# Two-block fp32 forward pass: attention sources normed beside the preceding projections, and the state-space mixer's sines and coefficients made beside the MLP and the input projection

## The chip, the cores and the metric

One core of a Trainium2 chip runs one program. The metric is the device time of one execution in microseconds, the median of several runs. The core has TensorE (PE; PEld are its weight loads), VectorE (DVE), ScalarE (ACT), GpSimd (POOL) and SyncE (SP), each with its own instruction stream; they meet through semaphores. 16 DMA engines move data between HBM and the on-chip memory SBUF. Matmul results land in PSUM.

## The reference, cut to what matters

Two blocks over 256 tokens of width 2048. The first is a mixer of long convolutions and a state-space scan with a squared-ReLU MLP (2048 to 8192 to 2048). The second, where the change lies:

```python
hn = rms_norm(h, norm_mix_g)
proj = hn @ w_in                                  # 2048 -> 3 x 1024: conv_a, conv_gate, ssm_u
yc = conformer_conv_group(conv_a, conv_gate, ...) # GLU, causal depthwise conv of 31 taps, norm, silu
ys = s5_group(ssm_u, lam_re, lam_im, log_dt, b, c, d, glu_w)
#   dt = exp(log_dt); lam_bar = exp(lam * dt); b_bar = ((lam_bar - 1) / lam) * b
#   states: scan of  s[t] = lam_bar * s[t-1] + b_bar u[t];  y = Re(c s) + d u;  gelu, gate
h = h + concat(rms_norm(yc), rms_norm(ys)) @ w_out
hn, mem_n = rms_norm(h, norm_mem_g), rms_norm(mem, mem_norm_g)
h = h + mem_cross_attention(hn, mem_n, w_q, w_kv, w_o)
h = h + peer(rms_norm(h, norm_ffn_g), ...)        # 16384 experts, top 16 of 8 heads
```

## The kernel before, in words

Activations lie feature-major: 16 tiles (KD) of 128 features by 256 tokens (T). A matmul keeps fp32 accuracy by splitting weights and activations into a rounded part and a rest (hi, lo).

`linear_stage` (line 603) is the dense stage. Per output tile there are 16 weight blocks of 128x128 in 4 quarters (a quarter is 128x512). SP streams 512 KB pairs of quarters into a ring of 4. ScalarE rounds a quarter into one of 4 slots (`make_hi`, L195) once TensorE has used the slot (`multiplied`); VectorE subtracts for the rest (`make_lo`, L202); TensorE multiplies (L793). So TensorE has at most four quarters, one tile, ahead. `split_and_take` sets the order on ScalarE and on VectorE: for tile n, first the four quarters of tile n + 1, then `take` of tile n, then the quarters of tile n + 2. In `take`, ScalarE copies half of the sum out of PSUM (L707), VectorE adds the other (L763) and runs `finish`: in the MLP's first layer a squared ReLU and its split (L1493 to L1495), after output projections x += and the sum of squares (L2202, L248, L249). Stages are separate blocks, with all engines meeting between them. A layer with `source` has its activations split first (L699, L751), one with `norm` also scaled (L726, L733), ahead of the first matmuls.

A `Beside` object is side work. Its hooks are called at fixed points: `tensor`, `scalar` and `after_tile` after each tile, `after_split(q)` after each `make_lo`, `last_vector` after the last tile, `issue` on GpSimd's queue. A layer with such an object is written out instead of looped. `split_and_take` counts quarters as `i * per + g`, with i the round of the layer and g from 4; each layer of a stage has a `split_and_take` of its own.

The second block in order: `in2` (8 + 8 + 8 tiles, the middle ones with a Sigmoid on ScalarE), `s5_setup_stage` (line 1507: exponentials, sines and some forty VectorE steps for the scan's coefficients b, c, r and turn), `local_mixers_stage` (line 1597), `glu`, group norm, `mix2_out`, `mem_q`, `mem_k`, values, attention, `mem_out`, experts. `mem_q` also loads mem and lets GpSimd sum its squares (`sum_tiles`, L595, L598) for `mem_k`'s norm.

In `local_mixers_stage`, for each of 8 tiles f: ScalarE makes phases (L1632, L1634), later their Sine (L1656), and 31 diagonal matrices of the convolution's taps (L1643); VectorE brings phases to one turn (L1719, L1720), rotates the inputs (L1737 to L1741), scans (L1748), rotates back with cosines (L1755), GpSimd with sines (L1622); TensorE makes inputs (L1673), outputs (L1687) and the 31 taps (L1698), in the order taps 0 to 11, inputs(f + 1), outputs(f - 1), taps 12 to 30.

Of the kernel before, what the change touches and what calls it, by code (L numbers as in the profile page):

```python
# [62 lines left out]
TWO_PI = 6.283185  # L63

# [60 lines left out]
class Core:  # L125


    def __init__(self, nc, ctx, dram):
# [8 lines left out]
        self.small = self.sb("small", [P, 4])  # L137
        self.mod = self.sb("mod", [P, 6 * KD, 2])
# [8 lines left out]
        self.moved, self.summed, self.shaped = (self.sem(f"tile_{n}") for n in ("moved", "summed", "shaped"))  # L147
        self.source_rounded, self.source_split = self.sem("source_rounded"), self.sem("source_split")
# [292 lines left out]

class ModulationBeside(Beside):
# [160 lines left out]
def linear_stage(core, name, layers, next_w, loads=(), begin_next=True, squares_of=None, beside=None):  # L603
# [21 lines left out]
    with ExitStack() as own:  # L625
# [42 lines left out]
        @block.gpsimd  # L668
        def _(pool):
            if beside is not None:  # L670
                beside.issue(pool)
            if squares_of is not None:
                pool.wait_ge(loaded, 16 * len(loads))
                sum_tiles(core, pool, loads[0][0], *squares_of)

# [268 lines left out]
def sine_steps(core, dve, x, k, bound_done):  # L944

    magic = 12582912.0
    c1, c2 = 6.28125, 2 * math.pi - 6.28125
    step = lambda ins: core.dve.step(dve, ins)
    step(dve.tensor_scalar(k, x, 1 / (2 * math.pi), magic, ALU.mult, ALU.add))
    step(dve.tensor_scalar(k, k, -magic, None, ALU.add))  # L950
    step(dve.scalar_tensor_tensor(x, k, -c1, x, ALU.mult, ALU.add))
    step(dve.scalar_tensor_tensor(x, k, -c2, x, ALU.mult, ALU.add))
    dve.tensor_scalar(x, x, 3.1415925, -3.1415925, ALU.min, ALU.max).then_inc(bound_done, 1)

# [7 lines left out]
def filter_stage(core, dft, filters):  # L962
# [6 lines left out]
    with ExitStack() as own:  # L969
# [10 lines left out]
        with nc.Block() as block:  # L980
# [61 lines left out]
            def _(dve):  # L1042
                step = lambda ins: core.dve.step(dve, ins)
                for n, bias in enumerate((b1, b2)):
# [4 lines left out]
                    sine_steps(core, dve, x, k, s["bounded"])  # L1049
# [372 lines left out]
def first_block(core):  # L1422
# [62 lines left out]
    with nc.sbuf_tensor("mlp_parts", [P, KD, 2, T], F32R) as parts:  # L1485
# [4 lines left out]
        with nc.sbuf_tensor("hidden", [P, MLP_TILES, 2, T], F32R) as hidden:  # L1490
            def squared_relu(dve, n, slots):
# [8 lines left out]
                    for c in range(chunks)]  # L1500
            linear_stage(core, "mlp", [Layer("w_mlp1", MLP_TILES, [parts], finish=squared_relu, steps=2), *down],
                         ("w_in_2", 0))
# [4 lines left out]
def s5_setup_stage(core, s5):  # L1507

    nc, dram = core.nc, core.dram
    s = {n: core.sem(f"s5_{n}") for n in ("loaded", "c_loaded", "cleared", "dt", "rate", "exp", "bounded", "sine")}
    W = HT * 64
    with ExitStack() as own:
        sb = lambda name, shape: own.enter_context(nc.sbuf_tensor(f"s5_{name}", shape, F32))
        rep = sb("rep", [P, 5, W])
        dt, e, trig, k = sb("dt", [P, W]), sb("e", [P, W]), sb("trig", [P, 2, W]), sb("k", [P, 2, W])
        kr, ki, t1, t2, inv = (sb(n, [P, W]) for n in ("kr", "ki", "t1", "t2", "inv"))
        sdt = sb("sdt", [P, PAIRS])
        sk = sb("sk", [P, PAIRS])  # L1520
        with nc.Block() as block:
            @block.sync
            def _(sp):
                sp.dma_start(rep[:], dram["s5_rep"]).then_inc(s["loaded"], 16)
                sp.wait_ge(s["cleared"], 1)

                for g in range(2):
                    for part in range(2):
                        sp.dma_start(s5.c[g * 64:(g + 1) * 64, part, :, g * 16:(g + 1) * 16],
                                     dram["s5_c"][part, g * 64:(g + 1) * 64]).then_inc(s["c_loaded"], 16)  # L1530

            @block.scalar
            def _(act):
                act.activation(sdt[:], core.prm["log_dt"], ACT.Exp).then_inc(s["dt"], 1)
                act.wait_ge(s["loaded"], 16)
                act.activation(dt[:], rep[:, 2, :], ACT.Exp).then_inc(s["dt"], 1)
                act.wait_ge(s["rate"], 1)
                act.activation(s5.r[:], s5.r[:], ACT.Exp)
                act.wait_ge(s["rate"], 2)
                act.activation(e[:], e[:], ACT.Exp).then_inc(s["exp"], 1)  # L1540
                act.wait_ge(s["bounded"], 1)
                act.activation(trig[:], trig[:], ACT.Sin).then_inc(s["sine"], 1)

            @block.vector
            def _(dve):
                step = lambda ins: core.dve.step(dve, ins)
                mul = lambda out, a, b: step(dve.tensor_tensor(out, a, b, ALU.mult))
                dve.memset(s5.c[:], 0.0).then_inc(s["cleared"], 1)
                dve.wait_ge(s["dt"], 1)
                dve.tensor_tensor(s5.r[:], core.prm["lam_re"], sdt[:], ALU.mult).then_inc(s["rate"], 1)  # L1550
                mul(s5.turn[:], core.prm["lam_im"], sdt[:])

                step(dve.tensor_scalar(s5.turn[:], s5.turn[:], 1 / (2 * math.pi), None, ALU.mult))
                step(dve.tensor_scalar(sk[:], s5.turn[:], MAGIC, None, ALU.add))
                step(dve.tensor_scalar(sk[:], sk[:], -MAGIC, None, ALU.add))
                step(dve.tensor_tensor(s5.turn[:], s5.turn[:], sk[:], ALU.subtract))
                dve.wait_ge(s["dt"], 2)
# [39 lines left out]
def local_mixers_stage(core, s5, proj, conv):  # L1597
# [8 lines left out]
    with ExitStack() as own:  # L1606
# [8 lines left out]
        with nc.Block() as block:  # L1615
# [9 lines left out]
            def _(act):  # L1625
# [28 lines left out]
                for f in range(HT):  # L1654
# [6 lines left out]
                    if f + 1 < HT:  # L1661
                        make_diag(f + 1)
# [788 lines left out]
```

## Time and profile before

| what | us |
|---|---|
| median of 3 runs (range) | 4411.7 (4409.6 to 4418.7) |
| profiled execution, whole | 4409.9 |
| its span | 4408.1 |
| MLP, first layer (64 tiles) | 357.8 |
| in2, first to last matmul (24 tiles) | 136.5 |
| from there to the mixers' first matmul | 35.9 |
| local mixers | 179.2 |
| mix2_out, first to last matmul (16 tiles) | 90.9 |
| mem_q, from mix2_out's last matmul to its own | 119.6 |
| mem_k, the same | 101.4 |

The table's stages are windows of one profiled execution. A row of a timeline gives start, duration, engine, line, operation, output and inputs; equal neighbours are merged (x8). "[0.75 <-PE ps L793]" is idle time before it and what ended it; PEq is a start of a stage. A group's busy time is not its cost: an engine that is not the limit of its stage may idle freely.

### The profile page before, as it was taken

The numbers are of one execution on the slowest core, as the hardware profiler recorded it, in microseconds if no ns is written. First come the engines' busy times: TensorE is split into PE (matmuls) and PEld (weight loads), VectorE is DVE, ScalarE is ACT, GpSimd is POOL, SyncE is SP. The second block draws the span as 40 slices with busy tenths as digits, with TensorE's granted clock in tenths as the row PEclk, the third lists the DMA queues.
The fourth block names the chain that finished last, engine by engine and source line by source line (L and its number), as shares of the span: only waits on it lengthen the run. The fifth ranks groups of instructions, "written<-read, shape, count | busy, mean of one in ns | idle before, by whom it ended". The sixth has DMA issues, their size and how long they took to land. (4 is left out here: it accounts for less than half of the span.)

```text
span 4408.1 us, 67179 instructions
## 1 busy us (share of the span) xinstructions
PE 3929.2 (89%) x21628; PEld 3230.7 (73%) x21628; DVE 2812.7 (64%) x5152; ACT 2086.3 (47%) x3815; POOL 172.7 (4%) x192
## 2 busy tenths in 40 slices
PE   6799968668999999858788999998889999999998
PEld 0466744557888888747577778877678888888887
DVE  0653445677777667669676556688776666666667
ACT  0442320234555555548544434444765555555554
POOL 3011100000000000002101000000000000000000
PEclk9899979888999999979898999899999999999999
DMA  9686710025666666430154545465246666666665
GB/s 335 233 302 242 263 60 0 1 91 149 190 190 187 189 190 186 140 106 1 39 180 144 167 138 154 152 188 180 77 137 205 205 204 187 189 187 189 189 188 161
DMA packets 203369, 717.71 MB, mean 163 GB/s; under 512 B 30263, under 2 KB 30296, under 8 KB 202456
## 3 DMA queue, kind: packets, MB, share of 16 engines
q1 hardware_dynamic: 181240, 633.41, 46.1%
q0 software_dynamic: 21984, 82.41, 5.2%
q8 instruction: 85, 1.39, 0.1%
q14 instruction: 60, 0.49, 0.0%
HBM read 707.35 MB, written 8.39 MB: 162 GB/s over the span
## 5 line engine op out<-in xcount | busy, mean ns | idle before, releaser
L202 DVE TENSOR_TENSOR weights_lo<-ring,weights_hi 128x512 fp32r<-128x512 f32 x2240 | 1522.6, 690 | 1025.3 <-ACT weights_hi L195 1011.3
L195 ACT ACTIVATE weights_hi<-ring 128x512 fp32r<-128x512 f32 x2240 | 1401.3, 631 | 1405.2 <-PE ps L793 1340.6
L793 PE MATMUL ps<-expert_parts,weights_hi 128*128 128x512 f32 x4224 | 1465.6, 394 | 34.5 <-DVE weights_lo L202 27.0
L793 PE MATMUL ps<-expert_parts,weights_lo 128*128 128x256 f32 x4224 | 1140.8, 280 | 0.0
L793 PEld LDWEIGHTS ps<-expert_parts,weights_hi 128*128 128x128 f32 x4224 | 780.1, 188 | 205.6 <-issue 36.5
L793 PEld LDWEIGHTS ps<-expert_parts,weights_lo 128*128 128x128 f32 x4224 | 796.6, 189 | 20.4
L793 PE MATMUL ps<-mlp_parts,weights_hi 128*128 128x512 f32 x1024 | 353.6, 394 | 16.0 <-PEq L552 16.0
L793 PE MATMUL ps<-hidden,weights_hi 128*128 128x512 f32 x1024 | 351.2, 392 | 0.0
L793 PE MATMUL ps<-att_parts,weights_hi 128*128 128x512 f32 x768 | 271.0, 400 | 29.6 <-DVE att_parts L751 28.1
L793 PE MATMUL ps<-h_parts,weights_hi 128*128 128x512 f32 x704 | 268.9, 409 | 10.0 <-DVE weights_lo L202 10.0
L793 PE MATMUL ps<-mlp_parts,weights_lo 128*128 128x256 f32 x1024 | 276.9, 281 | 0.0
L793 PE MATMUL ps<-hidden,weights_lo 128*128 128x256 f32 x1024 | 275.9, 280 | 0.0
L793 PEld LDWEIGHTS ps<-mlp_parts,weights_hi 128*128 128x128 f32 x1024 | 188.8, 189 | 54.7 <-issue 16.7
L793 PEld LDWEIGHTS ps<-hidden,weights_hi 128*128 128x128 f32 x1024 | 187.7, 188 | 37.6
L793 PE MATMUL ps<-att_parts,weights_lo 128*128 128x256 f32 x768 | 209.9, 283 | 0.0
L793 PEld LDWEIGHTS ps<-mlp_parts,weights_lo 128*128 128x128 f32 x1024 | 193.5, 189 | 5.4
L372 PE MATMUL ps<-ada_ring,silu_c 128*32 128x512 f32 x768 | 150.6, 628 | 51.5 <-DMA ada_ring<-in_w_ada 51.1
L793 PEld LDWEIGHTS ps<-hidden,weights_lo 128*128 128x128 f32 x1024 | 192.3, 188 | 5.4
L793 PE MATMUL ps<-h_parts,weights_lo 128*128 128x256 f32 x704 | 194.5, 285 | 0.0
L793 PEld LDWEIGHTS ps<-h_parts,weights_hi 128*128 128x128 f32 x704 | 134.9, 192 | 74.6 <-issue 45.0
L793 PEld LDWEIGHTS ps<-att_parts,weights_hi 128*128 128x128 f32 x768 | 144.0, 192 | 61.2 <-issue 32.3
L793 PEld LDWEIGHTS ps<-att_parts,weights_lo 128*128 128x128 f32 x768 | 147.6, 192 | 4.0
(440 smaller groups left out, 4859.0 us busy)
## 6 DMA issues: line engine op xcount, KB each, us to landing
ring<-in_w_mlp SPq DMA_DIRECT2D x256, 512.0 KB, 3.6
ring<-in_w_u SPq DMA_DIRECT2D x256, 512.0 KB, 4.2
ring<-in_w_v_tab SPq DMA_DIRECT2D x256, 512.0 KB, 3.7
ada_ring<-in_w_ada POOLq DMA_DIRECT2D x124, 512.0 KB, 6.3
ring<-in_w_mix SPq DMA_DIRECT2D x88, 512.0 KB, 5.4
ada_ring<-in_w_ada SPq DMA_DIRECT2D x68, 512.0 KB, 5.3
ring<-in_w_out SPq DMA_DIRECT2D x64, 512.0 KB, 3.7
ring<-in_w_in SPq DMA_DIRECT2D x48, 512.0 KB, 3.7
```

The costliest lines, as they stand in the source:

```text
L195: act.activation(core.hi[:, g % SLOTS], core.ring[:, slot, at:at + QUARTER], ACT.Copy).then_inc(core.rounded, 1)
L202: dve.tensor_tensor(core.lo[:, g % SLOTS], core.ring[:, slot, at:at + QUARTER], core.hi[:, g % SLOTS].bitcast(F32), ALU.subtract).then_inc ...
L372: mm = pe.matmul(self.core.ps[32 * j:32 * j + 32, self.bank(part), :], self.cond[:, k, :], self.ring[:, slot, (j % 2) * BANK:(j % 2 + 1) * ...
L793: mm = pe.matmul(out, part[:, g % SLOTS, k, :], moving, start=at == 0 and part is core.hi, stop=last and part is core.hi)
```

## The change

- `TurnsBeside` makes the mixers' sines beside the MLP's first layer (64 tiles): on even turns ScalarE makes the phases of one of 32 pairs, on odd turns VectorE rounds and subtracts and ScalarE takes the Sine; GpSimd's queue stores them to HBM, and the mixers' SP queue loads them per f.
- `MixerSetup` replaces `s5_setup_stage` and runs beside `in2`. GpSimd issues its loads (c in 16 parts) and clears c. `vector_first` and `vector_second` are generators spread over quarters by `after_split`.
- In the mixers VectorE makes the 31 diagonals of f = 0, ScalarE the rest; phases and Sine are gone from the stage.
- `NormBeside` makes a normed and split source beside another stage: that of mem (load, GpSimd squares, norm) beside `mix2_out` from tile 5, that of x beside `mem_k`. `mem_k` now runs ahead of `mem_q`, and neither has a source to make. Attention's scratch moves into an unused buffer.

```diff
+class NormBeside(Beside):
+    def tensor(self, pe, t):
+        if t == self.at:
+            if self.squared is not None:
+                pe.wait_ge(self.squared, 1)
+            pe.matmul(self.core.ps[:, self.BANK, 0:T], self.core.ones[:], self.squares, start=True,
+                      stop=True).then_inc(self.done["summed"], 1)
+    def scalar(self, act, turns):
+        t = turns[0] - self.at
...
+        if 2 <= t < 2 + KD // 2:
+            two = slice(2 * (t - 2), 2 * (t - 2) + 2)
+            act.wait_ge(self.done["scaled"], self.pairs + t - 1)
+            act.activation(self.parts[:, two, 0, :], self.scaled[:, two, :], ACT.Copy).then_inc(self.done["rounded"], 1)
+    def after_tile(self, dve, n):
+        t = n - self.at
...
+        if 1 <= t < 1 + KD // 2:
+            for k in (2 * (t - 1), 2 * (t - 1) + 1):
+                ins = dve.scalar_tensor_tensor(self.scaled[:, k, :], self.src[:, k, :], self.gain[:, k:k + 1], self.std,
+                                               ALU.mult, ALU.mult)
+            ins.then_inc(self.done["scaled"], 1)
+        if 3 <= t < 3 + KD // 2:
+            two = slice(2 * (t - 3), 2 * (t - 3) + 2)
+            dve.wait_ge(self.done["rounded"], self.pairs + t - 2)
+            dve.tensor_tensor(self.parts[:, two, 1, :], self.scaled[:, two, :], self.parts[:, two, 0, :].bitcast(F32),
+                              ALU.subtract)
...
+class TurnsBeside(Beside):
+    def issue(self, pool):
+        for u in range(PAIRS):
+            pool.wait_ge(self.done["trig"], u + 1)
+            pool.dma_start(self.saved[u // 4, :, u % 4], self.trig[:, u % 2]).then_inc(self.kept[u % 2], 16)
...
+    def scalar(self, act, turns):
+        n, small = turns[0], self.core.small
+        u = n // 2
+        if n % 2 == 0 and 0 <= u < PAIRS:
+            if u == 0:
+                act.wait_ge(self.done["rate"], 1)
+            if u >= 2:
+                act.wait_ge(self.kept[u % 2], 16 * (u // 2))
...
+        if n % 2 == 1 and 0 <= u < PAIRS:
+            act.wait_ge(self.done["phase"], u + 1)
+            act.activation(self.trig[:, u % 2], self.trig[:, u % 2], ACT.Sin, scale=TWO_PI).then_inc(self.done["trig"], 1)
+    def make_phase(self, dve, u):
...
+        dve.tensor_scalar(first, phases[:, 0], MAGIC, -MAGIC, ALU.add, ALU.add)
+        dve.tensor_scalar(second, phases[:, 1], MAGIC, -MAGIC, ALU.add, ALU.add).then_inc(done["step"], 1)
+        dve.wait_ge(done["step"], u + 5)
+        dve.tensor_tensor(phases[:, 0], phases[:, 0], first, ALU.subtract)
+        dve.tensor_tensor(phases[:, 1], phases[:, 1], second, ALU.subtract).then_inc(done["phase"], 1)
...
+class MixerSetup(Beside):
+    PART_A, PART_B = (2 * SLOTS, 10 * SLOTS), (12 * SLOTS, 22 * SLOTS)
+    COLUMNS_A, COLUMNS_B = 8400, 26000
...
+    def scalar(self, act, turns):
+        s = self.done
+        if 1 in turns:
+            act.wait_ge(s["loaded"], 16)
+            act.activation(self.dt[:], self.rep[:, 2, :], ACT.Exp).then_inc(s["dt"], 1)
+        if 10 in turns:
+            act.wait_ge(s["rate"], 2)
+            act.activation(self.s5.r[:], self.s5.r[:], ACT.Exp)
+            act.activation(self.e[:], self.e[:], ACT.Exp).then_inc(s["exp"], 1)
+            act.wait_ge(s["bounded"], 1)
+            act.activation(self.trig[:], self.trig[:], ACT.Sin).then_inc(s["sine"], 1)
+    def after_split(self, dve, q):
...
+        (a, b), (c, d) = self.PART_A, self.PART_B
+        if a <= q < b:
+            while self.spent * (b - a) < (q + 1 - a) * self.COLUMNS_A:
+                self.spent += next(self.first, self.COLUMNS_A)
...
+        if c <= q < d:
+            while self.spent * (d - c) < (q + 1 - c) * self.COLUMNS_B:
+                self.spent += next(self.second, self.COLUMNS_B)
+    def last_vector(self, dve):
+        for _ in self.second:
+            pass
...
@@ local_mixers_stage
-                make_turns(0)
-                make_diag(0)
+                make_diag(1)
...
+                for k in range(CONV31):
+                    dve.tensor_scalar(diag[:, 0, k, :], core.cst["ident"], core.prm["conv_w"][:, k:k + 1], None,
+                                      ALU.mult).then_inc(s["first_diag"], 1)
...
@@ second_block
-            ], ("w_glu", 0))
+            ], ("w_glu", 0), beside=MixerSetup(core, s5, sb3))
...
+            linear_stage(core, "mix2_out", [Layer("w_out_2", KD, [parts], finish=onto_stream(core), source=h, squares=True, steps=3)],
+                         ("w_k", 0), loads=[(mem[:], "mem")], squares_of=(mem_squares[:], mem_sum[:]),
+                         beside=NormBeside(core, mem, mem_sum[:, 0, :], core.prm["mem_norm"], mem_std[:], mem,
+                                           mem_parts, at=5, squared=core.loaded_squared))
...
+        linear_stage(core, "mem_k", [Layer("w_k", KD, [mem_parts], into=lambda n: k[:, n, :])], ("w_q", 0),
+                     beside=NormBeside(core, core.x, core.squares, core.prm["norm_mem"], std[:], h, parts))
+        linear_stage(core, "mem_q", [Layer("w_q", KD, [parts], into=lambda n: q[:, n, :])], ("w_v", 0))
```

## Rows read from the trace of the kernel before

**Rows 1.** the page, engines: busy us, share, instructions.

```profile
PE 3929.2 (89%) x21628; PEld 3230.7 (73%) x21628; DVE 2812.7 (64%) x5152; ACT 2086.3 (47%) x3815; POOL 172.7 (4%) x192
```

**Rows 2.** windows: length, busy by engine, clock, DMA share, GB/s.

```profile
1048.90:1406.70 357.80, 357.80 (x2048) 314.41 (x2049) 259.59 (x507) 178.70 (x318) 0.00 (x0) 0.99 0.61 188
1788.90:1925.40 136.50, 136.19 (x768) 119.07 (x768) 81.46 (x138) 77.91 (x135) 0.00 (x0) 0.98 0.58 177
1925.40:1961.30 35.90, 0.00 (x0) 0.02 (x1) 31.01 (x45) 6.14 (x10) 0.00 (x0) 0.53 0.30 51
1961.30:2140.50 179.20, 144.57 (x880) 113.29 (x880) 143.65 (x130) 144.71 (x328) 36.20 (x8) 0.89 0.00 1
2210.80:2301.70 90.90, 90.82 (x512) 79.54 (x512) 69.19 (x126) 45.29 (x81) 0.00 (x0) 0.98 0.60 182
2301.70:2421.30 119.60, 94.94 (x514) 81.93 (x514) 78.08 (x105) 49.32 (x85) 17.08 (x5) 0.87 0.48 158
2421.30:2522.70 101.40, 92.35 (x515) 80.27 (x514) 62.21 (x102) 49.35 (x85) 0.00 (x0) 0.95 0.52 166
2840.00:3123.00 283.00, 259.28 (x1440) 219.23 (x1438) 225.90 (x612) 127.94 (x270) 5.92 (x11) 1.00 0.60 188
```

**Rows 3.** timeline, one MLP tile: start, us, engine, line, op.

```profile
1201.49 0.63 ACT L195 ACTIVATE weights_hi<-ring 128x512 fp32r<-128x512 f32 x1 [0.75 <-PE ps L793]
...
1204.23 0.42 DVE L1495 TENSOR_TENSOR hidden<-mlp_sums,hidden 128x256 f32 x1
...
1204.57 1.29 DVE L202 TENSOR_TENSOR weights_lo<-ring,weights_hi 128x512 fp32r<-128x512 f32 x2
...
1207.05 0.63 ACT L195 ACTIVATE weights_hi<-ring 128x512 fp32r<-128x512 f32 x1 [0.76 <-PE ps L793]
```

**Rows 4.** timeline, start of the values stage.

```profile
2525.09 0.79 PE L1870 MATMUL ps<-weights_hi,att_parts 128*128 128x512 f32 x1 [2.38 <-PEq L625]
```

**Rows 5.** timeline, start of mem_q.

```profile
2308.28 3.26 DVE L733 SCALAR_TENSOR_TENSOR h_att<-x,params,mem_q_rstd 128x256 f32<-128x256 f32 x8
...
2312.59 12.66 DVE L733 SCALAR_TENSOR_TENSOR h_att<-x,params,mem_q_rstd 128x256 f32<-128x256 f32 x4
...
2313.14 7.20 POOL L595 TENSOR_TENSOR mem_squares<-mem 128x4096 f32<-128x4096 f32 x1 [176.54 <-DMA mem<-in_mem]
...
2325.17 3.36 DVE L751 TENSOR_TENSOR att_parts<-h_att,att_parts 128x1024 fp32r<-128x1024 f32 x1
```

**Rows 6.** timeline, gates, VectorE.

```profile
3132.86 1.11 DVE L2195 TENSOR_SCALAR gates_right<-consts,turned 128x128 f32<-128x128 f32 x4
```

**Rows 7.** waits of TensorE, experts_first: total, times, longest.

```profile
PE ps L793 <- DVE weights_lo L202: 23.6, 36, 1.3
```

**Rows 8.** timeline, ScalarE, a table load.

```profile
2826.03 1.28 ACT L2257 ACT_TABLE_LOAD   x1
```

**Rows 9.** timeline, end of in2 and the s5 setup, VectorE.

```profile
1926.70 0.41 DVE L763 TENSOR_TENSOR proj<-proj,ps 128x256 f32<-128x256 f32 x1
...
1939.86 1.41 DVE L1547 TENSOR_TENSOR s_t<-s_rep 128x512 f32<-128x512 f32 x2
...
1960.32 0.69 DVE L1591 TENSOR_SCALAR s_cc<-s_cc 128x1024 f32<-128x1024 f32 x1
```

**Rows 10.** timeline, local mixers.

```profile
1977.31 7.92 PE L1698 MATMUL ps<-mix_c,mix_diag 128*128 128x256 f32 x24 [13.90 <-ACT mix_diag L1643]
...
2023.51 12.02 ACT L1643 ACTIVATE mix_diag<-consts,small,params 128x128 f32<-128x128 f32 x31
...
2042.29 1.15 PE L1673 MATMUL ps<-proj,s_b 32*128 32x256 f32 x16
...
2045.23 8.47 PE L1698 MATMUL ps<-mix_c,mix_diag 128*128 128x256 f32 x38
...
2049.04 1.20 DVE L1719 TENSOR_SCALAR mix_p<-mix_trig 128x2048 f32<-128x2048 f32 x1
...
2050.27 2.29 DVE L1720 TENSOR_TENSOR mix_trig<-mix_trig,mix_p 128x2048 f32<-128x2048 f32 x1
```

More of the change, by code:

```diff
@@ L1500, in first_block @@
                     for c in range(chunks)]
-            linear_stage(core, "mlp", [Layer("w_mlp1", MLP_TILES, [parts], finish=squared_relu, steps=2), *down],
-                         ("w_in_2", 0))
+            with ExitStack() as beside:
+                turns = TurnsBeside(core, lambda name, shape: beside.enter_context(nc.sbuf_tensor(name, shape, F32)),
+                                    core.trig_saved)
+                linear_stage(core, "mlp", [Layer("w_mlp1", MLP_TILES, [parts], finish=squared_relu, steps=2), *down],
+                             ("w_in_2", 0), beside=turns)
@@ L1615, in local_mixers_stage, with _ @@
         with nc.Block() as block:
+            @block.sync
+            def _(sp):
+                for f in range(HT):
+                    if f >= 2:
+                        sp.wait_ge(s["out_c"], f - 1)
+                        sp.wait_ge(s["out_s"], f - 1)
+                    sp.dma_start(trig[:, f % 2], core.trig_saved[f]).then_inc(trig_landed[f % 2], 16)
             @block.gpsimd
@@ L1875, in values_stage, with attention_stage @@
     core.begun = True
[L1878 removed]
+def attention_stage(core, q, k, v, out, space):
     nc, ps = core.nc, core.ps
@@ L2238, in second_block @@
             glu_stage(core, y, parts, ("w_out_2", 0))
-        with nc.sbuf_tensor("out2_parts", [P, KD, 2, T], F32R) as parts, nc.sbuf_tensor("h_out2", [P, KD, T], F32) as h:
-            group_norm_stage(core, conv[:], y, h)
-            linear_stage(core, "mix2_out", [Layer("w_out_2", KD, [parts], finish=onto_stream(core), source=h, squares=True, steps=3)], ("w_q", 0))
-    with ExitStack() as attention:
-        sb = lambda name, shape, dt=F32: attention.enter_context(nc.sbuf_tensor(name, shape, dt))
-        q, k, v = sb("q", [P, KD, T]), sb("k", [P, KD, T]), sb("v", [P, TT, 4, BANK])
-        parts, h, mem = sb("att_parts", [P, KD, 2, T], F32R), sb("h_att", [P, KD, T]), sb("mem", [P, KD, T])
-        mem_squares, mem_sum = sb("mem_squares", [P, KD, T]), sb("mem_sum", [P, 1, T])
-        linear_stage(core, "mem_q", [Layer("w_q", KD, [parts], into=lambda n: q[:, n, :], source=h,
-                                         norm=Norm(core.x, core.prm["norm_mem"], squares=core.squares))], ("w_k", 0),
-                     loads=[(mem[:], "mem")], squares_of=(mem_squares[:], mem_sum[:]))
-        linear_stage(core, "mem_k", [Layer("w_k", KD, [parts], into=lambda n: k[:, n, :], source=mem,
-                                         norm=Norm(mem, core.prm["mem_norm"], squares=mem_sum[:, 0, :]))], ("w_v", 0))
-        values_stage(core, parts, v, ("w_o", 0))
-        attention_stage(core, q, k, v, parts)
```

308 lines of the change are left out of this document (191 added, 117 removed).

## The prediction

> **What bounds the kernel now.** I read the page's engine totals first, then busy time in windows whose edges are TensorE's first and last matmuls of a stage, then the order of instructions inside them. The total names the engine: TensorE is busy 89% of the span [rows 1]. The windows say where it is not the limit [rows 2]. In the MLP it is busy without a break, one tile of 16 weight blocks per 5.56 us (from one last rounding of a tile to the next, 1201.49 to 1207.05 [rows 3]); there, work on VectorE or ScalarE costs nothing until it makes the weight halves late. Four stretches are not of that kind: the s5 setup (1925.4 to 1961.3, TensorE at 0), the local mixers (179.2 us, 144.6 busy), and the starts of mem_q and mem_k (119.6 and 101.4 us for 16 tiles that take 16 x 5.56 = 89.0). Each part of the change shortens one of these and loads a dense stage instead, so I cost both sides. The profiled execution took 4409.9 us (span 4408.1), the median of the three runs 4411.7: I sum on the first and carry the difference over.
>
> **1. Attention sources (mem_q and mem_k).** Removed: the norm and split ahead of both stages. Their excess over 89.0 us is 30.6 + 12.4 = 43.0 us [rows 2]. Left is a plain hand-over: TensorE stood 2.4 us before the values stage, which has no source to make [rows 4], and a little longer, say 3.6, after a stage with x += and squares. A stage that starts after such a pause is 1.8 us (mix2_out, 90.9 - 89.0) to 3.1 us (in2, 136.5 - 24 x 5.56) over its steady pace; 2.6 each. So 3.6 + 2.4 + 5.2 = 11.2 remain, and 31.8 us go.
> Added in mix2_out, first the sum of squares of mem on GpSimd. It now runs beside VectorE's weight splits. In mem_q it held VectorE up: four scalings take 12.66 us while GpSimd's square and its first addition run, against 3.26 for the eight before, and a split of 1024 columns takes 3.36 against twice 0.69 for two of 512 (my reading: one VectorE instruction gets through per GpSimd instruction) [rows 5]. GpSimd is busy 17.1 us in five instructions [rows 2]. The load of mem leads the stage's queue as before, so the square starts as late as there, 7.8 us after a hand-over (2313.14 [rows 5] against 2301.7 + 3.6), in TensorE's first or second tile. VectorE gets some five instructions in 17 us and needs seven such ones per tile; TensorE has four weight quarters (5.56 us) ahead. Followed through: the third quarter of tile 1 is 3 us late, the fourth 3 more, the first of tile 2 4 to 5 more, which makes 11 us, and one restart at half clock, 2.6: 13.5 us (8 to 17; if these splits were not held, 0). Whether a split of 512 columns is held like the rows' forms, no row shows.
> The Trainium skill, page "SBUF — State Buffer", section "Who interferes with whom", says that a VectorE instruction with two SBUF inputs is shut out for the whole of a GpSimd instruction that reads SBUF. The two held forms agree with it; by it the splits, x += and the squares are held too, and the sum of a PSUM tile is not, which is how I took it.
> Second, NormBeside's VectorE work: per tile 2 scalings (0.41 each, 3.26 / 8) and one 512-column subtraction (0.69), 1.6 us onto 69.2 / 16 = 4.3, so 5.9 to 6.1 against 5.56 for the six tiles that hold both: 3 us (0 to 6). In mem_k, without x += and squares, the same load is under the pace: 0. Part 1: -31.8 + 13.5 + 3 = -15 us (-24 to -8).
>
> **2. Sines beside the first MLP layer (TurnsBeside).** Per pair of tiles: on an even turn ScalarE makes two phases; on the odd turn VectorE rounds and subtracts them after its own finish, and ScalarE waits for that ("phase"), then does a Sine of 128x512. Queued behind this wait on ScalarE is the rounding of the first weight quarter of the tile after next; behind that, VectorE's split and TensorE. In [rows 3] TensorE ends a tile at 1201.4, VectorE's finish at 1204.65, the split of the quarter in question at 1205.2, and TensorE needs it at 1207.0: 1.8 us spare. Now, after 1204.65: two adds of 128x256 (at least 0.26, which a 128x128 form takes in a row [rows 6], at most 0.42, as the subtraction; I take 0.3), two subtractions (0.36 to 0.42), and 0.05 for each hand-over: 1.35, to 1206.0; Sine 0.63 (ScalarE's time for 512 columns, L195 [rows 3]) to 1206.6; rounding 0.63; split 0.69: 1207.95. Late by 0.95 us, 32 times: 30 us, and 2.6 once for the rate chain in tile 0 and the first Sine's table load: 33 us (0.65 to 1.25 each: 23 to 43). The next tile has no such wait and does not win it back, since TensorE has no faster pace. That this coupling exists is seen in experts_first, where ScalarE's Gelu waits for VectorE in the same way: TensorE waits for weight halves 36 times, 23.6 us, longest 1.3 [rows 7], at a granted clock of 1.00 [rows 2]. The 32 saves on GpSimd's queue (256 KB each) hold no one: a slot is wanted again three tiles, 16.7 us, later.
>
> **3. Input projection (MixerSetup).** The first generator (6.5 us of VectorE over tiles 2 to 7, beside 3.2 per tile) fits. But its first step waits for ScalarE's exponential, which stands behind ScalarE's take of tile 1; queued behind VectorE's wait is the split of quarter 9: 1.7 us once. On turn 10 ScalarE does three activations (32, 512 and 1024 columns, 1.9 us by the 0.63 of 512) and two table loads of 1.28 [rows 8] between the sigmoid and the next rounding: 4.4 us against some 2.1 of cover, 2.3 us. Sum +4 (2 to 8).
> The table load's row is 1.28 us with no idle time before it [rows 8]. The Trainium skill, "ScalarE: Activation LUTs", section "What ACT_TABLE_LOAD costs", adds a drain of about 1.38 us to each switch; by it this part would be some 3 us more. The row shows no drain; I keep the row.
> The second generator is the surprise of the diff. It is meant for quarters 48 to 88, but the number that after_split gets is `i * per + g`, which starts again in each layer: with 8 tiles of 4 quarters it never passes 31. So part B is never met, and last_vector runs the whole second generator after the last tile, with nothing beside it. In the setup these steps stand from 1939.86 to 1961.01 [rows 9]: 21.15 us, which stay on the path. What goes is the stage change, the clearing, the load and the first half: 35.9 us from TensorE's last matmul to its next become 1.7 (to 1927.1, the end of the last take [rows 9]) + 21.15 + 0.3: -12.7 us (-14 to -10).
>
> **4. Local mixers.** Removed from ScalarE: 8 phases and one Sine per f; what is left is 12.0 of diagonals and 0.5 [rows 10]. VectorE loses 1.20 + 2.29 [rows 10] of 143.7 / 8 = 18.0 [rows 2] and keeps 14.5. TensorE's own cycle is 31 taps at 8.47 / 19 = 0.446, 13.8, and 2.94 for inputs and outputs (2042.29 to 2045.23): 16.8, now the longest. Start: the first diagonals move to VectorE, 31 after the 2.5 us product. At 0.26 each [rows 6] the first eight are there at 4.6 us, all at 10.5. Taps begin at 4.7 instead of 16.0 (1977.31 [rows 10]), and 12 of them take 7.9 at half clock, to 12.6; inputs(1) wait for VectorE's two products of 2.29, to 15.0; with inputs and 19 taps f = 0 ends at 24.7; seven more of 16.8 make 142.3; last outputs and skip 3.7: 146 against 179.2: -33 us (-37 to -25). The stored sines come by the SP queue, 1 MB per f, issued 10 us and more before they are wanted.
>
> **Sum.** -15 + 33 + 4 - 12.7 - 33 = -23.7: 4386.2 for the profiled execution, 4388.0 as a median.
>
> **Rivals.** (a) The Sine costs nothing: if VectorE's additions end 1 us sooner than I put together, part 2 is 3 and the time 4358. For: 1.8 us spare; against: a chain of four operations that adds up to 2.75. (b) Slower: the recurring pauses in the MLP drop TensorE's clock. Deciding point: a pause over 1.3 us, which left the clock at 1.00 in experts_first, up to the 2.4 after which the first matmul took 0.79 instead of 0.39 [rows 4]. If each of the 32 did, 2.6 us more each: +83, 4471. Against: my pause is 0.95. (c) GpSimd's squares do not hold the 512-column splits: 13.5 less, 4374.5. (d) The change does what it says and the coefficients lie inside the loops: -21.15, but ScalarE-bound sigmoid tiles with a VectorE step per quarter give back some 7.5: 4374.
>
> **How the numbers follow.** Forecast as summed, 0.72; (a) 0.10; (b) 0.06; (c) 0.08; (d) 0.04. A measurement of this kernel can tell 0.2% (8.8 us) from no change: the forecast case's own ends (the five ranges seldom all on one side) are 4370 to 4408, and 0.09 of it lies within 8.8 us of no change. Faster by over 0.2%: 0.84, within: 0.09, slower: 0.07. The range takes in (a), (c), (d) and a dearer part 2 and leaves (b) out: 4358 to 4412.
>
> **What would show it.** MLP up: TensorE's window 385 to 395 us instead of 357.8, its waits named on weights_lo, about 1 us, 32 times, ScalarE idle before Sine for VectorE. Before the mixers: about 23 us without a matmul, VectorE busy on s_t, s_kr, s_ki. Mixers about 146 us, no wait for mix_diag after f = 0. mix2_out about 105 us with a VectorE instruction of some 7 us; mem_k and mem_q some 95 each. It is wrong if the MLP window is under 370 or over 400, if coefficient steps stand among the splits of the input projection, or if mix2_out stays at 91.

## The result, and the profile after

The changed kernel takes 4372.1 us (median of four, 4369.1 to 4375.7) against 4411.1 for the kernel before: a ratio of 0.9908, with a 95% interval of 0.9895 to 0.9921. The forecast was 4388.0, in a range of 4358 to 4412. The profiled execution took 4375.7 us, span 4373.9, so the profiles differ by 34.2 us where the medians differ by 39.

Windows of the changed kernel (length, then busy time of TensorE, its weight loads, VectorE, ScalarE and GpSimd, then granted clock, DMA share, GB/s). In order: first MLP layer, input projection, the pause before the mixers, mixers up to the first matmul of the gated linear unit, mix2_out.

```profile
1047.00:1434.80 387.80, 366.02 (x2049) 314.50 (x2050) 292.39 (x637) 214.36 (x416) 16.85 (x31) 0.99 0.61 195
...
1818.20:1960.60 142.40, 138.34 (x768) 120.68 (x768) 87.21 (x146) 77.86 (x136) 9.54 (x15) 0.97 0.58 176
1960.60:1984.00 23.40, 0.31 (x5) 0.29 (x8) 21.49 (x32) 1.19 (x3) 0.00 (x0) 0.56 0.00 0
1984.00:2131.30 147.30, 136.40 (x881) 108.86 (x880) 123.61 (x147) 92.29 (x229) 36.33 (x8) 0.95 0.17 60
...
2195.40:2299.80 104.40, 95.72 (x514) 82.23 (x514) 94.07 (x150) 49.88 (x89) 16.98 (x5) 0.93 0.54 177
```

The mixers' window ends at another edge than that of [rows 2]. With the same edge the kernel before has:

```profile
1961.30:2146.80 185.50, 144.57 (x880) 113.29 (x881) 145.12 (x132) 149.91 (x332) 36.20 (x8) 0.89 0.01 3
```

Stretch by stretch:

| stretch | before | after | difference | forecast |
|---|---|---|---|---|
| first MLP layer | 357.8 | 387.8 | +30.0 | +33 |
| input projection | 136.5 | 142.4 | +5.9 | +4 |
| last matmul before the mixers to their first | 35.9 | 23.1 | -12.8 | -12.7 |
| mixers, to the gated linear unit | 185.5 | 147.6 | -37.9 | -33 |
| mix2_out | 90.9 | 104.4 | +13.5 | +16.5 |
| end of mix2_out to the first matmul of values | 223.4 | 189.6 | -33.8 | -31.8 |
| sum | | | -35.1 | -24.0 |

(The prediction rounds part 1 up to -15 and so sums to -23.7.) All the rest of the span differs by 0.9. What was given is seen in three places of the trace. First the MLP: a timeline of ScalarE, VectorE and TensorE over one odd tile (start, us, engine, line; in brackets the idle time before and what ended it).

```profile
1208.83 0.42 DVE L1554 TENSOR_TENSOR hidden<-mlp_sums,hidden 128x256 fp32r<-128x256 f32 x1
1209.17 0.29 DVE L1634 TENSOR_SCALAR params<-turn_trig 128x256 f32<-128x256 f32 x1
1209.37 0.28 DVE L1635 TENSOR_SCALAR turn_whole<-turn_trig 128x256 f32<-128x256 f32 x1
1209.69 0.43 DVE L1637 TENSOR_TENSOR turn_trig<-turn_trig,params 128x256 f32<-128x256 f32 x1
1210.04 0.42 DVE L1638 TENSOR_TENSOR turn_trig<-turn_trig,turn_whole 128x256 f32<-128x256 f32 x1
1210.49 0.63 ACT L1607 ACTIVATE turn_trig<-turn_trig 128x512 f32<-128x512 f32 x1 [3.27 <-DVE turn_trig L1638]
1211.03 2.18 ACT L200 ACTIVATE weights_hi<-ring 128x512 fp32r<-128x512 f32 x4
...
1211.44 0.40 PE L846 MATMUL ps<-mlp_parts,weights_hi 128*128 128x512 f32 x1
...
1211.67 2.50 DVE L207 TENSOR_TENSOR weights_lo<-ring,weights_hi 128x512 fp32r<-128x512 f32 x4 [1.22 <-ACT weights_hi L200]
1212.51 0.48 PE L846 MATMUL ps<-mlp_parts,weights_hi 128*128 128x512 f32 x1 [0.67 <-DVE weights_lo L207]
...
1212.83 0.28 PE L846 MATMUL ps<-mlp_parts,weights_lo 128*128 128x256 f32 x1
```

ScalarE stands idle for 3.27 us with four weight quarters to round, VectorE then for 1.22 with four to split, TensorE for 0.67. The waits over the whole layer (total, times, longest), TensorE's and ScalarE's, say that this is the rule:

```profile
PE ps L846 <- DVE weights_lo L207: 21.8, 32, 0.9
...
ACT turn_trig L1607 <- DVE turn_trig L1638: 100.3, 31, 3.3
```

Second, mix2_out, timeline of VectorE and GpSimd: three splits of 512 columns, of which two take 1.29 us in [rows 3], take 15.02 us while GpSimd makes its square and first additions.

```profile
2200.56 7.02 POOL L647 TENSOR_TENSOR mem_squares<-mem 128x4096 f32<-128x4096 f32 x1 [79.40 <-DMA mem<-in_mem]
2200.81 15.02 DVE L207 TENSOR_TENSOR weights_lo<-ring,weights_hi 128x512 fp32r<-128x512 f32 x3 [1.08 <-ACT weights_hi L200]
2207.65 9.33 POOL L650 TENSOR_TENSOR mem_squares<-mem_squares 128x2048 f32<-128x2048 f32 x3
2208.18 0.50 PE L846 MATMUL ps<-out_parts,weights_hi 128*128 128x512 f32 x1 [3.90 <-DVE weights_lo L207]
...
2209.32 0.61 PE L846 MATMUL ps<-out_parts,weights_hi 128*128 128x512 f32 x1
...
2213.12 0.80 PE L846 MATMUL ps<-out_parts,weights_hi 128*128 128x512 f32 x1 [2.98 <-DVE weights_lo L207]
...
2215.76 0.41 DVE L816 TENSOR_TENSOR mix_out_sums<-mix_out_sums,ps 128x256 f32<-128x256 f32 x1
```

Third, the pause before the mixers and their start, timeline of VectorE and TensorE. L1723 is the second generator's first step:

```profile
1962.29 1.41 DVE L1723 TENSOR_TENSOR s_t<-s_rep 128x512 f32<-128x512 f32 x2
...
1983.74 2.09 PE L1844 MATMUL ps<-proj,s_b 32*128 32x256 f32 x16 [23.09 <-PEq L677]
...
1986.14 6.15 DVE L1898 TENSOR_SCALAR mix_diag<-consts,params 128x128 f32<-128x128 f32 x31
...
1996.74 1.20 PE L1844 MATMUL ps<-proj,s_b 32*128 32x256 f32 x16 [1.94 <-DVE mix_p L1905]
1997.87 15.24 PE L1872 MATMUL ps<-mix_c,mix_diag 128*128 128x256 f32 x62
...
2015.98 13.66 PE L1872 MATMUL ps<-mix_c,mix_diag 128*128 128x256 f32 x62
2029.57 1.15 PE L1844 MATMUL ps<-proj,s_b 32*128 32x256 f32 x16
...
2046.09 1.15 PE L1844 MATMUL ps<-proj,s_b 32*128 32x256 f32 x16
```

### The profile page after: what moved, and what is told of

Same layout as the page of the kernel before. It is cut to its first block and busy times, and to the rows that moved or that the text cites. A ratio compares the mean times of both kernels' runs of the same rounds, so it can differ in the third digit from the quotient of the medians.

```text
span 4373.9 us, 65273 instructions
## 1 busy us (share of the span) xinstructions
PE 3928.3 (90%) x21628; PEld 3227.4 (74%) x21628; DVE 2817.6 (64%) x5302; ACT 2062.4 (47%) x3817; POOL 203.9 (5%) x242
## 5 line engine op out<-in xcount | busy, mean ns | idle before, releaser
L846 PE MATMUL ps<-mlp_parts,weights_hi 128*128 128x512 f32 x1024 | 361.5, 397 | 37.6 <-DVE weights_lo L207 21.8
L846 PE MATMUL ps<-att_parts,weights_hi 128*128 128x512 f32 x512 | 176.1, 392 | 4.0 <-PEq L677 2.5
L846 PE MATMUL ps<-in_parts,weights_hi 128*128 128x512 f32 x384 | 136.4, 401 | 11.1 <-DVE in_parts L804 7.1
L846 PEld LDWEIGHTS ps<-h_parts,weights_lo 128*128 128x128 f32 x704 | 135.4, 192 | 8.8
L846 PE MATMUL ps<-att_parts,weights_lo 128*128 128x256 f32 x512 | 138.0, 280 | 0.0
```

Of the source, the lines that this page charges most:

```text
L846: mm = pe.matmul(out, part[:, g % SLOTS, k, :], moving, start=at == 0 and part is core.hi, stop=last and part is core.hi)
```

## The experiments

Each edits the changed kernel and is measured against the kernel before. Three rounds or more give an interval; a kernel with one run is read by its windows.

| kernel | median us | ratio (95%) |
|---|---|---|
| sine_next_turn | 4344.5 | 0.9855 (0.9838 to 0.9871) |
| coefs_in_loops | 4352.9 | 0.9869 (0.9853 to 0.9886) |
| small_mem_sum | 4360.6 | 0.9890 (0.9873 to 0.9906) |
| no_mem_sum | 4359.9 | one run |
| phases_longer | 4427.5 | one run |
| first_taps | 4373.5 | one run |
| coefs_spread | 4345.4 | one run |
| combined_more | 4314.1 | 0.9786 (0.9769 to 0.9802) |
| combined_less | 4307.3 | 0.9767 (0.9753 to 0.9780) |
| combined_moved | 4302.8 | 0.9760 (0.9746 to 0.9773) |

### sine_next_turn: the Sine off the tile that makes its phases

```diff
+        if n % 2 == 0 and u > 0:
+            self.sine(act, u - 1)
         if n % 2 == 0 and 0 <= u < PAIRS:
...
-        if n % 2 == 1 and 0 <= u < PAIRS:
+        if n == 2 * PAIRS - 1:
+            self.sine(act, u)
```

> Each pair's Sine is issued on ScalarE one turn later (turn 2u+2 instead of 2u+1, ahead of that turn's two phases); every instruction of the sines is still there, on the same engines, and the saves too. Theory (the Sine's place: ScalarE waits for VectorE's subtraction inside the same tile, and the rounding of the next weight quarter is queued behind that): the 32 waits of ScalarE for the phase go to nothing but the last, TensorE's waits for weights_lo in the first MLP layer (21.8 us, 32 times) go to under 3 us, its window falls from 387.8 to 358 to 361, and the time from 4372.1 to about 4344. Rival 1 (the added work itself is what the MLP cannot hide, VectorE's 1.2 us and ScalarE's 1.2 us per pair): the window stays at 380 or more. Rival 2 (the 8 MB of saves on GpSimd's queue delay the weight loads): the same, 385 or more, with TensorE's waits led back to DMA.

Measured: TensorE's waits in the layer fell from 21.8 us in 32 to 1.5 in 2, the window to 359.5, the time to 4344.5. Window of the layer:

```profile
1043.00:1402.50 359.50, 358.50 (x2049) 314.89 (x2050) 295.15 (x637) 221.67 (x416) 17.22 (x31) 0.99 0.66 210
```

TensorE's waits in it:

```profile
PE ps L846 <- DVE weights_lo L207: 1.5, 2, 0.9
```

VectorE and ScalarE are as busy as before (295 and 222 us against 292 and 214), and GpSimd's queue stores as much. So the added work and the saves together cost at most 1.7 us (359.5 against 357.8 before): 28 of the 30 us were the place of one wait. Both rivals fall, and rival (a) of the prediction, by which the Sine costs nothing where it stands.

### phases_longer: the same chain made longer

```diff
+        for r in range(5):
+            dve.tensor_scalar(first, phases[:, 0], MAGIC, -MAGIC, ALU.add, ALU.add).then_inc(done["step"], 1)
+            dve.wait_ge(done["step"], 6 * u + r + 5)
         dve.tensor_scalar(first, phases[:, 0], MAGIC, -MAGIC, ALU.add, ALU.add)
...
```

> Ahead of each pair's phases VectorE makes five more rounding steps of 128x256, each waited for by the next (0.29 us and a hand-over of some 0.05 each): the chain from VectorE's finish to ScalarE's Sine grows by 1.5 to 1.7 us, 32 times. Theory (TensorE is late by the chain less a cover that is fixed): its pause of 0.68 us becomes 2.2 to 2.4 us, and the first MLP layer's window 387.8 + 32 x 1.6 = 439 with a clock that stays at 0.99. Rival (b) of the prediction (a pause of more than 1.3 us drops the clock): each restart costs some 2.6 us more, the window passes 500 and the granted clock of the stretch falls under 0.9. If the pauses came from anything else than this chain, the window stays under 400.

Measured, the layer's window:

```profile
1047.30:1490.40 443.10, 370.49 (x2049) 318.32 (x2050) 338.39 (x792) 214.43 (x416) 16.78 (x31) 0.98 0.53 171
```

TensorE's waits in it:

```profile
PE ps L846 <- DVE weights_lo L207: 72.6, 32, 2.3
```

Two restarts in the timeline:

```profile
1208.28 0.47 PE L846 MATMUL ps<-mlp_parts,weights_hi 128*128 128x512 f32 x1 [2.31 <-DVE weights_lo L207]
...
1237.19 0.77 PE L846 MATMUL ps<-mlp_parts,weights_hi 128*128 128x512 f32 x1 [2.32 <-DVE weights_lo L207]
```

A pause grew from 0.68 us (21.8 / 32) to 2.27 (72.6 / 32), by 1.59. The chain from VectorE's finish to its last subtraction took 2.84 us (1203.39 to 1206.23) instead of 1.21, 1.63 more: the cover is fixed and every further us is paid. The window is 443.1 and not the 439 expected, and TensorE is busy 4.5 us longer than in the changed kernel. Some of that is the clock: 31 of the pauses last 2.31 to 2.35 us. After 28 of them the first matmul takes 0.47 us, where steady ones take 0.39, and full clock lasts; two restart at half clock (one at 1237.19, with 0.77 us), and once the clock falls to half 2 us after the restart. Over the layer it is 0.98. Rival (b), by which each such restart costs 2.6 us, is refuted; that such a pause can cost the clock is not.

### small_mem_sum and no_mem_sum: GpSimd's sum of squares in mix2_out

```diff
-    step(pool.tensor_tensor(scratch, src, src, ALU.mult))
+    for k in range(KD):
+        step(pool.tensor_tensor(scratch[:, k, :], src[:, k, :], src[:, k, :], ALU.mult))
...
+    for k in range(2, KD):
+        step(pool.tensor_tensor(out[:, 0, :], out[:, 0, :], scratch[:, k, :], ALU.add))
```

> The sum of squares of mem on GpSimd is made in 31 instructions of 256 columns instead of five of up to 4096 (the same additions but for their order). Theory (while a GpSimd instruction runs, VectorE's split of 512 columns is held until it ends, so one VectorE instruction passes per GpSimd instruction, however long): with 0.5 to 0.7 us per GpSimd instruction a split waits for at most that, VectorE loses some 0.3 to 0.5 us on each of about 20 instructions and not 15 us on three; the window of mix2_out falls from 104.4 to 93 to 97, and the time by 7 to 11 us, to 4361 to 4365. Rival (what counts is GpSimd's busy time, 17 us and now more, in which VectorE runs slower in proportion): the window stays at 102 or more.

```diff
-                sum_tiles(core, pool, loads[0][0], *squares_of)
+                core.pool.step(pool, pool.memset(squares_of[1], 1.0))
```

> The sum of squares of mem is left out: GpSimd fills its result with ones by one small memset, so the attention's keys and values are normed by a constant; the load of mem, NormBeside's own work and all else stay. The window of mix2_out then shows NormBeside's work alone: 91 to 95 us by the theory (the hold costs the rest of the +13.5: I put 13.5 to the hold and 3 to NormBeside), against 100 or more if VectorE's added scalings and subtractions are what costs.

Window of mix2_out in small_mem_sum:

```profile
2189.50:2284.60 95.10, 92.23 (x514) 79.74 (x514) 89.50 (x150) 49.83 (x89) 27.36 (x31) 0.98 0.58 194
```

and in no_mem_sum:

```profile
2196.90:2288.30 91.40, 91.40 (x514) 79.73 (x514) 79.98 (x150) 49.82 (x89) 0.31 (x1) 0.98 0.60 202
```

Without the sum the stage takes 91.4 us: the hold costs 104.4 - 91.4 = 13.0, and NormBeside's own work 0.5 over the 90.9 of [rows 2]. That work leaves VectorE no idle time in the later tiles. From one sum of a tile to that of the fifth tile after it, in no_mem_sum:

```profile
2256.14 0.41 DVE L816 TENSOR_TENSOR mix_out_sums<-mix_out_sums,ps 128x256 f32<-128x256 f32 x1
...
2284.32 0.41 DVE L816 TENSOR_TENSOR mix_out_sums<-mix_out_sums,ps 128x256 f32<-128x256 f32 x1
```

That is 28.18 / 5 = 5.64 us per tile against TensorE's 5.56, and TensorE does not wait.

In small pieces the sum costs 3.7, with the window in the 93 to 97 expected. GpSimd is then busy for 27.4 us instead of 17.0 and VectorE loses less, so it is not GpSimd's busy time that counts but the length of one instruction. Timeline of small_mem_sum beside the pieces:

```profile
2194.36 14.12 POOL L648 TENSOR_TENSOR mem_squares<-mem 128x256 f32<-128x256 f32 x16 [79.16 <-DMA mem<-in_mem]
...
2200.65 4.05 DVE L207 TENSOR_TENSOR weights_lo<-ring,weights_hi 128x512 fp32r<-128x512 f32 x4
2204.62 0.41 DVE L815 TENSOR_TENSOR mix_out_sums<-mix_out_sums,ps 128x256 f32<-128x256 f32 x1
...
2205.53 0.72 DVE L253 TENSOR_TENSOR mix_out_sums<-x 128x256 f32<-128x256 f32 x1
```

Four splits take 4.05 us where they took 2.50 in the MLP; a square of 128x256 with both inputs in SBUF takes 0.72 instead of the 0.43 it takes where no GpSimd instruction runs; the sum whose second input is in PSUM keeps its 0.41. The Trainium skill, "SBUF — State Buffer", section "Who interferes with whom", says that a VectorE instruction with two SBUF inputs contends with a GpSimd instruction that reads SBUF, and one with at most one does not. These rows agree. The x += between them, which has two SBUF inputs as well, took 0.42 to 0.53 in the four tiles: hardly held, and why is open.

### coefs_in_loops, coefs_spread: the second generator into the loops

```diff
     def after_split(self, dve, q):
+        if q < self.passed:
+            self.base += 4 * HT
+        self.passed = q
+        q += self.base
```

> The quarter's number that the setup steps go by is counted on over the three layers of the input projection instead of starting again in each; so the second generator runs on VectorE between the splits of tiles 12 to 21 and not after the last tile. Theory (rival (d) of the prediction): the 23.1 us between the last matmul of the projection and the first of the mixers become 2 to 3, and the projection's window grows from 142.4 to some 150, because a sigmoid tile leaves VectorE little room and a reciprocal of 512 columns (3.3 us) goes between two splits: net -13 us, about 4358. Rival 1 (VectorE's slack of some 2.3 us per tile takes all 21 us over ten tiles): the window stays under 145 and the net is -19 or more, 4352. Rival 2 (stalls that drop TensorE's clock): the window passes 160 and less than 5 us are left of the gain.

coefs_spread adds to that:

```diff
-    PART_A, PART_B = (2 * SLOTS, 10 * SLOTS), (12 * SLOTS, 22 * SLOTS)
+    PART_A, PART_B = (2 * SLOTS, 6 * SLOTS), (12 * SLOTS, 22 * SLOTS)
...
-        if 10 in turns:
+        if 7 in turns:
...
-        step(dve.reciprocal(inv[:], inv[:]))
+        for c in range(4):
+            part = slice(c * W // 4, (c + 1) * W // 4)
+            step(dve.reciprocal(inv[:, part], inv[:, part]))
```

> On top of coefs_in_loops: ScalarE's two exponentials and its Sine come on turn 7, the last tile before the sigmoid layer, instead of turn 10, with the first generator squeezed into tiles 2 to 5, and the reciprocal of 512 columns is made in four instructions of 128 between other splits. coefs_in_loops showed two waits of TensorE that these two should explain: 2.44 us at 1889.94 (turn 10: two table loads and a Sine of 1024 columns) and 2.14 us at 1899.34 (behind the reciprocal of 3.35 us). Theory: both go, and with them the half-clock restarts; the projection's window falls from 147.9 to 139 to 142. Rival (the waits come from the sum of VectorE's work on sigmoid tiles, and only move): 145 or more.

Window of the projection in coefs_in_loops:

```profile
1815.90:1963.90 148.00, 140.90 (x768) 121.96 (x768) 105.26 (x173) 77.03 (x137) 9.55 (x15) 0.96 0.56 170
```

and in coefs_spread:

```profile
1811.70:1955.20 143.50, 138.05 (x768) 119.51 (x768) 105.35 (x176) 73.97 (x135) 9.54 (x15) 0.98 0.57 175
```

In coefs_in_loops the pause before the mixers fell from 23.1 to 2.0 us and the projection grew by 5.6. The window, 148.0, is near the 150 of the theory; the net, 19 us, is that of rival 1. By windows it is 21.1 - 5.6 + 1.7 = 17.2: TensorE now enters the mixers at full clock (its first 16 matmuls there take 1.15 us instead of 2.09) and they too are 1.7 us shorter. The other 2 us are in no window that I compared. coefs_spread, where the two waits of 2.44 and 2.14 us are gone, has 4.5 us back; which of its changes does it, the earlier turn or the reciprocal in four, no run separates. It still has five waits, 5.2 us in all, longest 1.6, and at 143.5 it stands between theory (142) and rival (145): undecided, and the reason for combined_moved.

### first_taps: the diagonals of f = 0 shared

```diff
+                for k in range(12):
+                    act.activation(diag[:, 0, k, :], core.cst["ident"], ACT.Identity, scale=core.prm["conv_w"][:, k:k + 1],
...
                     dve.tensor_tensor(p2[:], bu, sin(f), ALU.mult).then_inc(s["turned"], 1)
+                    if f == 0:
+                        for k in range(12, CONV31):
+                            dve.tensor_scalar(diag[:, 0, k, :], core.cst["ident"], core.prm["conv_w"][:, k:k + 1], None,
```

> In the local mixers, for f = 0, ScalarE makes the diagonals of taps 0 to 11 ahead of those of f = 1, and VectorE those of taps 12 to 30 behind its two products instead of ahead of them. Theory (what holds the mixers' first pass is VectorE's order: 31 diagonals, 6.15 us, ahead of the two products that inputs(1) waits for): the second group of inputs starts some 7 us after the first instead of 13.0 us (1996.74 - 1983.74), TensorE saves 3 to 5 us in the first pass, and the stretch from the first inputs to the gated linear unit's first matmul falls from 147.6 to 143 to 145. Rival (ScalarE's diagonals of f = 1, now 4.7 us later, or VectorE's later passes take its place as the limit): 147 or more.

TensorE's groups of inputs in first_taps:

```profile
1984.74 2.09 PE L1847 MATMUL ps<-proj,s_b 32*128 32x256 f32 x16 [23.09 <-PEq L677]
...
1994.07 1.15 PE L1847 MATMUL ps<-proj,s_b 32*128 32x256 f32 x16 [0.78 <-DVE mix_p L1907]
...
2011.59 1.40 PE L1847 MATMUL ps<-proj,s_b 32*128 32x256 f32 x16 [2.79 <-DVE mix_p L1907]
```

The second group comes after 9.3 us instead of 13.0 (I had said some 7); the third waits 2.79 us for VectorE's products of f = 1, and the outputs behind it run slower (1.08, 1.93 and 0.75 us instead of 0.64, 1.05 and 0.61). The stretch is 146.7 instead of 147.5, where the theory had 143 to 145. My theory of where the first pass is held was right, but most of the gain is given back one pass later: the rival, within 0.3 us of its 147.

### All together

> All mends together: the Sine one turn later, the quarter counted on with the exponentials on turn 7 and the reciprocal in four, the sum of squares of mem in pieces of 256 columns, and the diagonals of f = 0 shared. If the gains are in separate stretches and add up: from the changed kernel's 4372.1, -28 (sine_next_turn), -19 (coefs_in_loops), -6 (coefs_spread over it), -9 (small_mem_sum, by its window), -3 (first_taps): 4307, between 4300 and 4316, some 2.3% under the kernel before. If they shared a limit, the sum would fall short: 4325 or more.

It took 4314.1, some 7 us over what I expected. The mixers had lost in it: 148.1 us against 145.9 in coefs_in_loops. So the next kernel leaves the diagonals as they were, and a further one keeps the generator out of most sigmoid tiles:

> combined_more without the sharing of the diagonals of f = 0 (VectorE makes all 31 again). first_taps brought 0.8 us alone (147.5 to 146.7 us from the first inputs to the gated linear unit's first matmul), and in combined_more this stretch took 148.1 us against 145.9 in coefs_in_loops. Theory (VectorE's products of f = 1 set the start, and a TensorE that gets there sooner waits 2.6 to 2.8 us and restarts at half clock; in combined_more the first sines landed 2.3 us late for the earlier products besides): without the sharing the stretch is 145 to 146 us again and the time some 2 us below combined_more, 4310 to 4313. Rival (the difference between the two kernels is from elsewhere): the stretch stays at 148.

```diff
-    PART_A, PART_B = (2 * SLOTS, 6 * SLOTS), (12 * SLOTS, 22 * SLOTS)
-    COLUMNS_A, COLUMNS_B = 8400, 26000
+    PART_A, PART_B = (2 * SLOTS, 6 * SLOTS), (17 * SLOTS, 23 * SLOTS + 2)
+    PART_C, COLUMNS_C = (6 * SLOTS, 10 * SLOTS), 5180
+    COLUMNS_A, COLUMNS_B = 8400, 14400
...
```

> combined_less with the second generator kept out of the eight sigmoid tiles but for their first two: its squares, addition and reciprocals (5.4 us) run over tiles 6 to 9, which depend on no exponential, the rest over tiles 17 to 23. Theory (a sigmoid tile keeps VectorE waiting for ScalarE between the sum and the copy, so that a step among its splits comes out late; coefs_spread still had 5 waits of 5.2 us and a window of 143.5): the projection's window falls to 138 to 141 and the time by 3 to 5 us against combined_less. Rival (the rest is too dense in seven tiles: 15 us of steps on some 2.4 us of slack per tile): the waits move to the last layer and the window stays at 143 or more.

combined_less took 4307.3, below the 4310 to 4313 expected, with the mixers' stretch at 145.9 again; that its time is below combined_more's is not clear, as their intervals overlap. combined_moved took 4302.8. Its windows, projection and mixers:

```profile
1785.70:1925.50 139.80, 136.91 (x768) 119.31 (x768) 105.34 (x176) 75.00 (x134) 9.55 (x15) 0.98 0.59 180
1927.50:2073.40 145.90, 135.13 (x880) 108.17 (x880) 123.77 (x147) 92.58 (x229) 36.37 (x8) 0.96 0.17 61
```

The same VectorE time as in coefs_spread (105.3 us), and a window 3.7 us shorter (3.5 shorter than in combined_less, 143.3), in the 138 to 141 expected; TensorE's waits for weight halves there fell from 5.2 us in five to 2.5 in two. The place among the tiles mattered, not the sum. The intervals of these last two kernels overlap, so that it is the window and not the time that carries this. combined_moved is 2.4% under the kernel before. By medians it is 69 us under the changed one; by the two ratios, each against runs of the kernel before beside it, 65 (0.0148 of 4411). By windows, 28 are the first MLP layer, 23.7 the way from the start of the projection to the mixers (165.5 to 141.8), 1.7 the mixers and 9 mix2_out, together 63; the rest, 3 to 7 us, I ascribe to nothing.

## Why the prediction was right, point by point

All six terms have the sign forecast for them. The time came out 16 us below the forecast: 10.5 in the profiles, because five of the six errors lie to one side, and 5 that the medians differ by more than the profiles do. Most terms hold by their mechanism; where a term was hit by parts that miss in opposite ways, it is said below.

- **MLP, 30.0 for 33.** The mechanism is shown by sine_next_turn and phases_longer, and the recurring part was right: 30.0 / 32 = 0.94 us per pair where I had 0.95. In steady work the next matmul starts 0.23 us after one of 512 columns, while that still runs (0.39). Behind the one at 1211.44, the last before the pause, the next was due at 1211.67 and started at 1212.51, 0.84 late, and had its own successor after 0.32 us (1212.83) instead of 0.23: 0.93. VectorE's four steps took 1.21 us and not 1.35, which made up for the slow first matmul that I had not put in: two small errors of opposite sign. The profile divides this otherwise, 21.8 us of idle time (0.68 each) and 8.2 us more of busy time (366.0 against 357.8 [rows 2]). What failed to come is the 2.6 once in tile 0: the longest of the 32 waits is 0.91.
- **Projection, 5.9 for 4.** Two waits were forecast, 1.7 and 2.3 us; TensorE waited twice for weight halves, 1.63 and 2.43 us. On turn 10 ScalarE took 4.4 us from the first table load to the end of the Sine (1886.38 to 1890.80), as summed. What I left out is the slow restart: TensorE's busy time rose from 136.2 to 138.3, and after the wait of 2.43 us its first matmul took 0.77 us, half clock.
- **Setup, 12.8 for 12.7.** The second generator never met its quarters and ran whole after the last tile, as read from the code (1962.29 to 1983.43); VectorE is busy 21.5 of the 23.4 us, TensorE at 0. With the quarter counted on, rival (d) would have been true: I put -13.7 on that, coefs_in_loops measured -19.3 by medians and -17.2 by windows.
- **Mixers, -37.9 for -33.** TensorE's cycle is the bound, as forecast. The sum had 146 us to the end of the last skip; measured are 141.2 (1983.74 to 2124.95), in three parts. Tile 0 ended 24.1 us in for 24.7: a diagonal took 0.20 us on VectorE (6.15 / 31), not the 0.26 of [rows 6], so that inputs(1) started 13.0 us in and not 15.0, but behind the wait of 1.94 us the taps ran in part at half clock (granted clock 0.65 from 1996.7 to 2000.0), and 62 of their matmuls took 15.24 us for the steady 13.66, so that most of the 2 us was lost. The seven further tiles took 114.7 us for 117.6: a cycle is 16.5 (groups of inputs at 2029.57 and 2046.09), not 16.8, and the last has no inputs after it. The last outputs and skip took 2.5 us for 3.7, a figure that in the kernel before held matmuls at half clock after a wait of 4.32 us.
- **mix2_out, 13.5 for 16.5.** The hold was 13.0 for 13.5, and it holds 512-column splits, which no row of before had shown; rival (c) is refuted. That its sum is so near is in part luck: against no_mem_sum it is 8.7 us of TensorE's waits, for the 11 that I followed through, and 4.3 of added busy time (95.7 against 91.4), for one restart of 2.6; behind each of three waits it ran at half clock for a while (0.50 to 0.53 granted). NormBeside cost 0.5 for 3. The term that failed is its density: I added durations to 5.9 to 6.1 us per tile, 0.3 to 0.5 over TensorE's pace, but instructions in a row overlap (four splits take 2.49 us, not 4 x 0.69), and a full tile took VectorE 5.64, or 0.08 over the pace.
- **Attention sources, -33.8 for -31.8.** Two errors of opposite sign: TensorE's pauses ahead of mem_k and mem_q took 4.28 and 2.46 us, 6.7 for the 6.0 forecast, and the slow starts behind them 2.4 for 5.2. No run took this part alone; it rests on the two traces.

The Trainium skill, "ScalarE: Activation LUTs", section "What ACT_TABLE_LOAD costs", weighed in the prediction, would add a drain to each switch of tables. On turn 7 of coefs_spread the second table load starts at 1867.55, with 1.28 us to the activation that follows at 1868.84, and none of it idle:

```profile
1867.16 0.36 ACT L760 ACTIVATE in_sums<-ps 128x256 f32<-128x256 f32 x1
1867.55 1.28 ACT L2404 ACT_TABLE_LOAD   x1
1868.84 0.42 ACT L2404 ACTIVATE in_sums<-in_sums 128x256 f32<-128x256 f32 x1
```

Here, as in [rows 8], the trace does not agree with the drain.

## What to carry to other kernels

Work moved beside a dense stage was nearly free as work here and dear as a wait: of the 43.5 us that the MLP layer and mix2_out gave up (30.0 and 13.5), 28.3 came back with one Sine issued a turn later and 9.3 with a sum cut into small GpSimd instructions, with the same work done. Before placing a step, ask which wait stands ahead of the next weight quarter on the same queue, put the consumer a tile later than the producer, and cut what runs on GpSimd into pieces of a split's size (the same for a long VectorE instruction, a reciprocal of 3.35 us, is likely but was not tried alone). Where a counter decides the place of a step, check in the instruction order that it gets there: here a counter that starts again in each layer left 21 us exposed.

## What the runs showed of the hardware that I had not expected

- The length of a pause does not by itself tell what TensorE's clock does after it. In phases_longer one pause of 2.32 us was followed by a first matmul of 0.77 us, half clock, and 28 of 2.31 to 2.32 us by one of 0.47. In mix2_out the first matmul after 3.90 us took 0.50, but 1.1 us later they took 0.61 (granted clock 0.52 from 2209.3 to 2210.1); after the next pause, 2.98 us, the first took 0.80 at a granted clock of 0.50, against the steady 0.39. My deciding point for rival (b), a single length, was of the wrong kind.
- A short pause costs more than its idle time. In the MLP 32 pauses of 0.68 us idle cost 0.94 us each: the last matmul before a pause has no successor to overlap with (0.40 us, where the next starts 0.23 in), and the first after it is 0.09 slower to its successor.
- Beside each other both engines are slower: a GpSimd square of 128x256 takes 0.61 us at the start of the kernel, in the same form, and 0.83 in the median beside VectorE's splits, while a split goes from 0.63 to 1.01 (2.50 / 4 and 4.05 / 4).
